# Attention in a fused fp32 block: P turned in 32x32 blocks by VectorE, multiplied with V on four row quarters, output product in two parts

## The reference, cut to what matters

```python
# 32 query heads and 4 key/value heads of width 64; windows of 128 positions, two query blocks
scores = q @ k.T                       # band: key position in (query - 128, query]
m = maximum(max(scores), sink)
p = exp(scores - m)
probs = p / (sum(p) + exp(sink - m))   # P
out = probs @ v                        # per head: [256, 64]
x = x + out.reshape(256, 2048) @ w_o
x = x + swiglu(rms_norm(x))            # gate, up: 2048 -> 5632; down: 5632 -> 2048
```

## Time and profile before

| | us |
|---|---|
| median of three runs | 1934.54 |
| the profiled execution, its own time | 1934.93 |
| its span, first to last instruction | 1933.1 |

### The profile page before, as it was taken

How to read it: one execution, slowest core, us unless ns; L and a number is a source line. 1 busy time by engine, 2 the same in 40 slices (tenths; PEclk the granted TensorE clock), 3 DMA queues, 4 the chain that set the end, 5 groups by cost and what they waited for, 6 DMA issues and landing times.

```text
span 1933.1 us, 26528 instructions
## 1 busy us (share of the span) xinstructions
PE 1918.3 (99%) x9668; PEld 1573.9 (81%) x9668; DVE 1302.0 (67%) x1852; ACT 1075.4 (56%) x1405; POOL 555.6 (29%) x616
## 2 busy tenths in 40 slices
PE   7999999999999999999999999999999999999999
PEld 6888878888888888888887778888888888888887
DVE  5799967556878888886667877555555555554443
ACT  6444466456768686875467775544444444443332
POOL 0899852306050423302400106023222222220000
PEclk9999999999999999999999999999999999999999
DMA  8666656666555555555654445666666666666665
GB/s 298 198 188 189 181 163 194 187 197 185 163 165 163 147 180 152 174 150 179 195 186 134 129 145 180 199 195 195 193 190 192 191 196 191 193 194 195 192 193 161
DMA packets 183006, 352.45 MB, mean 182 GB/s; under 512 B 11776, under 2 KB 12288, under 8 KB 182912
## 3 DMA queue, kind: packets, MB, share of 16 engines
q1 hardware_dynamic: 181488, 350.68, 60.1%
q10 hardware_dynamic: 1424, 0.53, 0.1%
HBM read 349.07 MB, written 2.10 MB: 182 GB/s over the span
## 4 chain that ended last, share of the span: by engine, by line
PE 79%; issue 6%; DVE 4%; ACT 4%; POOL 4%; DVEq 1%; POOLq 1%; ACTq 0%; DMA 0%
PE acc L508 26%; PE acc L510 25%; PE acc L509 25%; POOL kb L448 2%; POOL kf L448 1%; ACT E L959 1%; DVEq L1132 1%; DVE w_lo L1146 1%; PE T L490 1%; ACT w_hi L761 1%; PE T L709 1%; PE T L698 1%; POOLq L443 0%; DVE E L1366 0%; DVE E L1358 0%
## 5 line engine op out<-in xcount | busy, mean ns | idle before, releaser
L1146 DVE TENSOR_TENSOR w_lo<-raw,w_hi 128x1024 fp32r<-128x1024 f32 x568 | 699.1, 1234 | 538.3 <-ACT w_hi L761 530.7
L761 ACT ACTIVATE w_hi<-raw 128x1024 fp32r<-128x1024 f32 x656 | 688.4, 1057 | 601.3 <-PE acc L510 577.9
L508 PE MATMUL acc<-w_hi,h_hi 128*128 128x512 f32 x1888 | 745.2, 395 | 9.9 <-DVE w_lo L1146 9.7
L510 PE MATMUL acc<-w_hi,h_lo 128*128 128x512 f32 x1888 | 736.8, 390 | 0.0
L509 PE MATMUL acc<-w_lo,h_hi 128*128 128x512 f32 x1888 | 736.8, 390 | 0.0
L508 PEld LDWEIGHTS acc<-w_hi,h_hi 128*128 128x128 f32 x1888 | 355.3, 188 | 89.8 <-issue 14.2
L510 PEld LDWEIGHTS acc<-w_hi,h_lo 128*128 128x128 f32 x1888 | 355.2, 188 | 74.4
L509 PEld LDWEIGHTS acc<-w_lo,h_hi 128*128 128x128 f32 x1888 | 355.5, 188 | 71.2
L479 POOL COPY fT<-fq 32x256 f32<-32x256 f32 x176 | 110.8, 630 | 388.2 <-DVE fq L1599 381.3
L417 POOL TENSOR_TENSOR w_lo<-raw,w_hi 128x1024 fp32r<-128x1024 f32 x80 | 190.3, 2404 | 76.4 <-ACT w_hi L761 76.3
L1219 DVE SCALAR_TENSOR_TENSOR T<-vpad,feat,T 128x256 f32<-128x256 f32 x464 | 182.4, 478 | 0.0
(11 more groups left out here) (237 smaller groups left out, 1564.2 us busy)
## 6 DMA issues: line engine op xcount, KB each, us to landing
raw<-in_hgrn_w_in_dram SPq DMA_DIRECT2D x160, 512.0 KB, 3.7
raw<-in_conv_w_in_dram SPq DMA_DIRECT2D x96, 512.0 KB, 4.2
raw<-in_ffn_w_gate_dram SPq DMA_DIRECT2D x88, 512.0 KB, 4.4
raw<-in_ffn_w_up_dram SPq DMA_DIRECT2D x88, 512.0 KB, 4.5
raw<-in_ffn_w_down_dram SPq DMA_DIRECT2D x88, 512.0 KB, 4.8
raw<-in_attn_w_qkv_dram SPq DMA_DIRECT2D x40, 512.0 KB, 4.1
raw<-in_conv_w_out_dram SPq DMA_DIRECT2D x32, 512.0 KB, 4.6
raw<-in_hgrn_w_out_dram SPq DMA_DIRECT2D x32, 512.0 KB, 4.6
```

Of the source, the lines that this page charges most:

```text
L508: nc.tensor.matmul(o, hi[:, kt, a], w_hi[:, slot, kk, :], start=kt == 0, stop=False)
L510: last = nc.tensor.matmul(o, lo[:, kt, a], w_hi[:, slot, kk, :], start=False, stop=kt == p.chunks * CK - 1)
L761: A(w_hi[:, slot, :, :], raw[:, slot, :, :], ACT.Copy).then_inc(hi_ready, 1)
L1146: TT(w_lo[:, slot, :, :], raw[:, slot, :, :], rounded(w_hi[:, slot, :, :]), ALU.subtract).then_inc(split_ready, 1)
```

## The change

1. **P is scaled by two other engines.** `scale_p` becomes `inverse` (VectorE, reciprocal alone), `scale_first` (GpSimd, query block 0, four operations of 256 elements a group, behind its chunk e+9) and `scale_second` (ScalarE, query block 1, eight copies of 128x256 with a scale, at e+10+i).
2. **P is turned by VectorE** within 32x32 blocks (`p_turn(i)`, two transposes of 128x384 at e+11+i) straight into `PT`, which now holds all 8 heads. `turn_p` and `p_copy` go.
3. **V lies in all four row quarters.** `v_rows` on GpSimd copies V so that each quarter of the partitions holds all 8 blocks of 32 keys: 16 copies of 32x512, behind `k_turn`. `kvtok` now shares memory with PT.
4. **`mix_v(g)`** is one step for all 8 heads: 60 fp32 products (32 rows, 64 columns of the array, 128 moving columns), in turn over 4 row quarters and 2 column halves, at tick e+16 (g = 3: e+14). It waits for `masked` of group g+1, since it writes all of T.
5. **`y_out_hi(g)`** (four copies of 128x256 on ScalarE) moves to tick e+18 (g = 3: e+16), **`y_low(g)`** (four on VectorE) to e+19 (g = 3: e+17).
6. **att_out in two parts**: eight segments of 4 chunks, first the upper 1024 rows of `w_o` for the four column groups, then the lower. `first_part` (VectorE) adds the first to x. Column groups are complete after chunks 19, 23, 27 and 31 of att_out. `late` and `lead` go.

```diff
     for name, iters, per, more in (
             ("conv_ab", 4, 2, {}), ("conv_z", 1, 4, {}), ("conv_out", 1, 4, {}), ("hgrn", 4, 4, {}),
-            ("hgrn_z", 1, 4, {}), ("hgrn_out", 1, 4, {}), ("kv_q", 1, 5, {}), ("att_out", 1, 4, {"lead": 2}),
+            ("hgrn_z", 1, 4, {}), ("hgrn_out", 1, 4, {}), ("kv_q", 1, 5, {}), ("att_out", 1, 8, {"chunks": CPG // 2}),
             ("gate_up", FJ, 2, {}), ("down", 1, 4, {"chunks": FCH})):
...
-        kvtok = sb(yl2, "kvtok", [P, TB, GC])
+        PT = sb(yl2, "PT", [P, 8, 3 * P])
+        kvtok = PT[:, :, :].rearrange("p a b -> p (a b)")[:, 0:TB * GC].rearrange("p (a b) -> p a b", a=TB)
         aq = sb(yl2, "aq", [P, TB, GC])
+        vrows = apad[:, 3:5, :, :].rearrange("p a b (c d) -> p (a b c) d", d=KVH * HD)
...
-        PT = sb(yl2, "PT", [P, 4, 3 * P])
...
+            def v_rows():
+                pool.wait_ge(a_ev, 1)
+                pool.wait_ge(a_T, 1)
+                for a in range(4):
+                    for b in range(4):
+                        nc.gpsimd.tensor_copy(vrows[a * QUARTER:(a + 1) * QUARTER, b::4, :], kvtok[b * QUARTER:(b + 1) * QUARTER, :, KVH * HD:])
+                nc.gpsimd.drain().then_inc(a_rows, 1)
+
+            def scale_first(g, i):
+                pool.wait_ge(a_inv, 4 * g + i + 1)
+                nc.gpsimd.tensor_tensor(sm[:, 2 * i:2 * i + 2, P:2 * P], sm[:, 2 * i:2 * i + 2, P:2 * P],
+                                        ast[:, 6, 2 * i:2 * i + 2].unsqueeze(2).to_broadcast([P, 2, P]), ALU.mult).then_inc(a_n0, 1)
+            v_rows()
...
+                    i = n - ph["kv_q"].chunk0
+                    if i % 8 == 1:
+                        for p in range(4):
+                            scale_first(i // 8 - 3, p)
...
                 pe.wait_ge(a_cp, 2)
                 if g:
-                    pe.wait_ge(a_ptc, 8 * g)
+                    pe.wait_ge(a_sm, 8 * g)
+                if g > 1:
+                    pe.wait_ge(a_lo, 4 * (g - 1))
...
+            def mix_v(g):
+
+                pe.wait_ge(a_rows, 1)
+                pe.wait_ge(a_pt, 4 * g + 4)
+                pe.wait_ge(a_sm, 8 * (min(g + 1, 3) + 1))
+                if g:
+                    pe.wait_ge(a_lo, 4 * g)
                 for tb in range(TB):
-                    for h in (2 * i, 2 * i + 1):
-                        o = T[HD * (h % 2):HD * (h % 2) + HD, 2 + i // 2, (i % 2) * S + tb * P:(i % 2) * S + S]
-                        w = PT[:, h % 4, 2 * P:3 * P] if tb else PT[:, h % 4, 0:2 * P]
-                        last = nc.tensor.matmul(o, v(tb), w, start=tb == 0, stop=tb == 1)
+                    for step in range(5):
+                        for a in range(4):
+                            blocks = range(4 + a, 4 + a + 5) if tb else range(a + 1)
+                            if step >= len(blocks):
+                                continue
+                            b, r = blocks[step], slice(a * QUARTER, (a + 1) * QUARTER)
+                            key = b if b < 4 else b - 4
+                            for c in range(2):
+                                o = T[c * HD:(c + 1) * HD, a, :].rearrange("p (i t q) -> p i t q", t=TB, q=QUARTER)[:, 0:4, tb, :]
+                                w = PT[r, c:8:2, b * QUARTER:(b + 1) * QUARTER]
+                                last = nc.tensor.matmul(o, vrows[r, key, g * HD:(g + 1) * HD], w, start=step == 0, stop=step == len(blocks) - 1)
                 last.then_inc(a_o, 1)
...
-                for i in range(4):
-                    at.put(e + 8 + i, lambda g=g, i=i: turn_p(g, i))
-                    at.put(e + 9 + i, lambda g=g, i=i: mix_v(g, i))
+                at.put(e + 16 if g < 3 else e + 14, lambda g=g: mix_v(g))
...
+            def scale_second(g, i):
+                act.wait_ge(a_inv, 4 * g + i + 1)
                 for h in (2 * i, 2 * i + 1):
...
+                    s = probabilities(h)[1]
+                    last = A(s, s, ACT.Copy, scale=ast[:, 6, 8 + h:8 + h + 1])
+                last.then_inc(a_n1, 1)
+
+            def y_out_hi(g):
+                act.wait_ge(a_o, g + 1)
+                for i in range(4):
+                    A(by_quarters(y_hi, 4 * g + i), mixed(i).rearrange("p a (b i) -> p a b i", b=TB), ACT.Copy).then_inc(a_hi, 1)
...
-                        at.put(e + 11 + i, lambda g=g, i=i: p_copy(g, i))
-                    for b in range(2):
-                        at.put(e + 13 + 2 * b, lambda g=g, b=b: y_out_hi(g, b))
+                        at.put(e + 10 + i, lambda g=g, i=i: scale_second(g, i))
+                    at.put(e + 18 if g < 3 else e + 16, lambda g=g: y_out_hi(g))
...
+            def first_part(name, k):
+
+                dve.wait_ge(chunk_used, ph[name].done(0, k))
...
+                    if ph[name].in_parts:
+                        at.put(ph[name].last[k] + 3, lambda k=k: first_part(name, k))
...
+            def inverse(g, i):
 
                 dve.wait_ge(a_p, 4 * g + i + 1)
                 l, inv = (ast[:, r, :].rearrange("p (a b) -> p a b", a=2)[:, :, 2 * i:2 * i + 2] for r in (4, 6))
-                V.reciprocal(inv, l)
-                settle()
+                V.reciprocal(inv, l).then_inc(a_inv, 1)
+
+            def p_turn(g, i):
+
+                dve.wait_ge(a_n0, 4 * g + i + 1)
+                dve.wait_ge(a_n1, 4 * g + i + 1)
+                if g:
+                    dve.wait_ge(a_o, g)
+                else:
+                    dve.wait_ge(a_rows, 1)
                 for h in (2 * i, 2 * i + 1):
...
+                    last = V.transpose(PT[:, h, :], sm[:, h, P:4 * P])
+                last.then_inc(a_pt, 1)
+
+            def y_low(g):
+                dve.wait_ge(a_hi, 4 * g + 4)
+                for i in range(4):
+                    low(by_quarters(hy_lo, 4 * g + i), mixed(i).rearrange("p a (b i) -> p a b i", b=TB), by_quarters(y_hi, 4 * g + i), a_lo)
...
+                    at.put(e + 8, lambda g=g: masked(g, 1)).put(e + 8, lambda g=g: inverse(g, 0)).put(e + 8, lambda g=g: maxima(g, 1))
                     for i in range(1, 4):
-                        at.put(e + 9 + i, lambda g=g, i=i: scale_p(g, i))
-                    for b in range(2):
-                        at.put(e + 14 + b, lambda g=g, b=b: y_low(g, b))
+                        at.put(e + 9 + i, lambda g=g, i=i: inverse(g, i))
+                    for i in range(4):
+                        at.put(e + 11 + i, lambda g=g, i=i: p_turn(g, i))
+                    at.put(e + 19 if g < 3 else e + 17, lambda g=g: y_low(g))
```

More of the change, by code:

```diff
@@ L78, with __init__ @@
 class Phase:
-    def __init__(self, iters, per_iter, chunk0, pair0, uses0, chunks=CPG, lead=0):
+    def __init__(self, iters, per_iter, chunk0, pair0, uses0, chunks=CPG, columns=4):
         self.chunk0, self.pair0, self.uses0 = chunk0, pair0, uses0
@@ L88, in __init__, with segment, row @@
         self.uses_per = [sum(self.pair(k) == p for k in range(per_iter)) for p in range(2)]
-        head = [(k, c) for cs in (range(chunks - 4), (chunks - 4, chunks - 3), (chunks - 2,), (chunks - 1,))
-                for k in range(lead) for c in cs]
-        self.seq = head + [(k, c) for k in range(lead, per_iter) for c in range(chunks)]
+        self.seq = [(k, c) for k in range(per_iter) for c in range(chunks)]
         self.last = {k: i for i, (k, c) in enumerate(self.seq) if c == chunks - 1}
-        self.chunks = chunks
+        self.chunks, self.in_parts, self.columns = chunks, per_iter == 2 * columns, columns
         self.chunk1 = chunk0 + iters * len(self.seq)
         self.uses1 = [uses0[p] + iters * self.uses_per[p] for p in range(2)]
+    def segment(self, k):
+        return k + self.columns if self.in_parts else k
+    def row(self, k, c):
+        return self.chunks * (k // self.columns) + c if self.in_parts else c
     def pair(self, k):
@@ L106, in done, with first_reads @@
         return self.base(j) + self.last[k] + 1
+    def first_reads(self, k):
+        return k == 0 or self.in_parts and k == self.columns
     def use(self, j, k):
@@ L112, in end @@
     def end(self, k):
-        return self.last[k] + 1
+        return self.last[self.segment(k)] + 1
 def phases():
@@ L386, in _ @@
             stream("kv_q", 0, lambda k: (t["attn_w_qkv_2"][0], (k - 1) * GC if k else D))
-            stream("att_out", 0, lambda k: (t["attn_w_o_2"][0], k * GC))
+            stream("att_out", 0, lambda k: (t["attn_w_o_2"][0], k % 4 * GC))
             with sp.Fori(0, FJ) as j:
@@ L498, in stream @@
                     n, slot, _ = slots(base, i)
-                    if need is not None and k == 0:
-                        need(c)
+                    row = p.row(k, c)
+                    if need is not None and p.first_reads(k):
+                        need(row)
                     if c == 0 and not (isinstance(p.use(j, k), int) and p.use(j, k) == 0):
@@ L505, in stream @@
                     for kk, tb in ((0, 0), (1, 0), (0, 1), (1, 1)) if ends else ((0, 0), (0, 1), (1, 0), (1, 1)):
```

(6 more changed lines are left out.)

69 lines of the change are left out of this document (22 added, 47 removed).

## The result

The changed kernel takes 1962.37 us (median of four runs, 1960.96 to 1962.55); the kernel before took 1934.78 beside it. The ratio is 1.0141, 95% interval 1.0128 to 1.0153: 27.6 us slower, where 29.8 were predicted. The profiled execution's span is 1960.7 us, 27.6 more than before's.

A forecast was written before the change was run, and what follows sets the result against it. TensorE was taken as the bound, with a second chain across engines 0.8 us behind that would take over. Terms 0.7 + 14.6 + 1.2 + 4.9 + 8.4 = 29.8 us on 1934.54 gave 1964.3, range 1948 to 1983.

The forecast's parts named there:

- group 0 to 1, without clock: First period from scores to scores, with no y_out_hi in the way: 33.7 us against 33.0, +0.7.
- groups 1 to 2 and 2 to 3, without clock: Two later periods: ScalarE's wait at y_out_hi, copies and scaling lengthen each from 32.75 to 40.0 us, +7.3 twice.
- clock at three waits: TensorE's waits for rope at q_turn drop its clock: 0 to 2.8 us each, taken as 2.8 each, 8.4.
- behind scores(3): After the last scores, late w_lo of chunks 51 to 53 makes TensorE 1.2 us later at chunk 58.
- behind att_out: After the output products, TensorE waits for x_lo(2) behind GpSimd's three moves: 4.9 us, or 2.8 with moves at 10.90.
- S: Start of scores(1), 1064.11 in the earlier trace; times in the softmax chain are counted from it.
- M: Length of one mix_v on TensorE: 2.25 us if all eight tiles overlap, 6.5 if row quarters do not.
- rival one: In mix_v, row quarters do not overlap, M = 6.5: +17 us, 1981 in all; chance 0.14.
- upper bound: Top of the main case's bounds for the whole kernel: 1975 us, with M of 3 and clock lost at two more waits.
- Z: End of column group 0 in att_out; x_lo(2) was forecast at Z+49.4, wanted by TensorE at Z+44.5.
- Rival two: ScalarE's y_out_hi finds mix_v nearly done, so the chain grows by copies alone: +12 us, 1946; chance 0.09.
- the faster rival: Softmax groups: TensorE's sum decides if the second chain stays under 28.5 us: 1918 to 1923; chance 0.07.

The follow-up runs named there:

- idle-filling run: Changed kernel with 24, 32 and 20 useless 512-column matmuls on TensorE ahead of the wait in q_turn(1), (2) and (3); 1957.18 us, ratio 1.0116.
- run by quarters: Changed kernel with the same 60 products of each mix ordered one row quarter after another instead of in turn; 1971.42 us, ratio 1.0185.
- version with ScalarE's order: Changed kernel with late mix copies, GpSimd scaling P's second half, TensorE turning column group 2, V's copies split, q_out earlier, exps(3) later; 1931.06 us, ratio 0.9984.
- bursts of 240: Changed kernel with the 60 products of each mix_v made twice, the second pass writing the same result over; 1982.25 us, ratio 1.024.
- last ordered version: The version with ScalarE's order, with VectorE's third turn of P ahead of y_low and the fourth pair's reciprocal right behind the rope; 1930.63 us, ratio 0.9977.

## Why the prediction was right, point by point

| term | predicted | trace |
|---|---|---|
| ahead of scores(0) | 0 | 2.1 |
| group 0 to 1, without clock | 0.7 | 0.4 |
| groups 1 to 2 and 2 to 3, without clock | 14.6 | 13.5 |
| clock at three waits | 8.4 | 5.2 |
| behind scores(3) | 1.2 | 0.9 |
| behind att_out | 4.9 | 5.3 |
| sum | 29.8 | 27.5 |

The column on the right is stretch after less stretch before, with the clock's part from the idle-filling run's periods or, the same, q_turn to scores less 3.78 (5.71, 5.48 and 5.39 us).

**The mechanism.** Scores to scores were forecast at 33.7, 40 and 40 and are 33.4, 39.5 and 39.5 once the clock's part is taken out. The wait ahead of y_out_hi was forecast at 4.9 us, from S+8.87 to S+13.75; it is 4.96 and ends at S+13.93. VectorE goes on behind the rope at S+35.8, forecast 36.15. The experiments that moved only that step and y_low behind it moved the time both ways, so this cause is shown, not argued.

**M.** 2.25 forecast, 2.17 measured; rival one (row quarters don't overlap) is out. The run by quarters shows that it would have been right by half, had the products stood in the plain order.

**The copies.** Four copies of 128x256 from PSUM take 1.07 us to the next step, 0.27 each, not 0.36: the earlier trace rows had them with a second operand (`feat`). That is 0.4 of the 0.5 us by which each period came out shorter; the rest is the turn's start, for which the sum had 0.1 us behind VectorE's and the trace has nothing. The scaling (0.81 a pair) and p_turn(2) (0.95) came as priced.

**The clock, the term furthest off.** I carried 2.8 us over from the start of the span to each wait (by my own figures, 6.39 less 3.41, it is 3.0). The waits were 7.0, 8.9 and 4.9 us, and the loss 1.9, 1.7 and 1.6: the granted clock came back within the first chunk, while at the span's start fifteen matmuls ran low. The clock fell behind the 4.0 us for hy_lo as well (0.66 from 1131 to 1136), at no price, since q_turn(3) waited all the same. Behind the wait in gate_up I took nothing; 3.55 us of idle time brought the clock down there too, and the loss was 1.7 (PEclk 0.66 over 5 us). In all 6.9 for 8.4: two errors that offset one another by half. How near 29.8 comes to 27.6 is in part luck: 3.2 us too much here and 1.1 too much in the two long periods stand against 2.1 ahead of scores(0), for which I had nothing. The upper bound was mis-added too: 3 us for the mix and twice 2.8 for the clock make 1973, not 1975.

**v_rows.** I took 0 of the bounds 0 to 1, having read that VectorE's steps last no longer beside GpSimd's moves of 32x256. That reading was wrong: in the trace of before four w_lo in a row beside such moves start every 1.34 us and take 1.41 each, not 1.22, and a move beside a w_lo takes over three times as long:

```profile
1200.33 5.43 DVE L1146 TENSOR_TENSOR w_lo<-raw,w_hi 128x1024 fp32r<-128x1024 f32 x4
L432 POOL COPY apad<-aq x48: 387/398/1462, 1168.3 to 1204.7; 32x256 f32<-32x256 f32 x48
1169.62 1.43 POOL L432 COPY apad<-aq 32x256 f32<-32x256 f32 x1
```

(The second row has the shortest, the middle and the longest of the 48 moves in ns.) Beside copies of 32x512 three of the rope's operations took 1.09 instead of 0.68 and three of w_lo 1.35 to 1.66 instead of 1.23; v_rows costs 1.2, outside of my bounds. The other 0.8 us ahead of scores(0) stand by k_turn already, ahead of anything that the change touches; among the traces here k_turn starts anywhere from 1008.9 to 1011.0.

**The end.** 4.9 forecast, all of it wait; it is 3.6 of wait and 1.7 of clock. My terms add up to Z+49.05, not Z+49.4, so the forecast should have been 4.6. The three moves take 10.81, 11.13 and 12.05 us instead of the earlier trace rows's 10.90, 12.07 and 11.83, 0.8 less together, which is most of the rest. Their length is set by VectorE: undisturbed moves start every 0.43 us, so 16 would take 6.9 us, an estimate from these rows; four or five of each 16 take 1.3 to 1.5, each of them beside a w_lo. Rival two (ScalarE's order hurts less, 1946) and the faster rival (1918 to 1923, "a chain that is not one") didn't come; but the latter's number can't be had cheaply either: with the order mended the three groups take 32 us on the mean, not TensorE's 28.5.

## What to carry to other kernels

When an engine's program is written out in order, a step that reads another engine's result delays all that stands behind it: put it by the time at which its input is there, not by the time at which it is wanted. Before taking work from the engine that is busy for 99%, add up the next chain: here it stood 0.8 us behind, and of the some 16 us that TensorE was relieved of by its own sum (its busy time fell by 13.1 us, to 1905.2, in the version with ScalarE's order), nothing reached the time, and no more than 0.2% of it once steps on ScalarE, VectorE and GpSimd had been moved too.

## What the runs showed of the hardware

- **Tiles over row quarters and column halves work side by side.** Interleaved over four row quarters and two column halves, 120 records of 128 columns start every 18 ns on average; ordered by quarter, every 35 ns; both for fp32 products in two passes. One record takes 109 ns, so six of the eight tiles are at work on the mean, an estimate from these rows; the tiles of the longest quarter have 18 records each, 1.96 of the 2.17 us.
- **A long burst runs dry.** 231 small records passed at 17.5 ns each, then TensorE stood 2.08 us for no reason that a row shows; all four bursts of 240 did it, somewhere behind record 182 to 239, and 120 at a time don't show it. The cause is open.
- **GpSimd's copies and VectorE's operations on two tiles hold each other up.** The copy that started 0.02 us behind a w_lo, and that w_lo:

```profile
1021.97 1.23 DVE L1178 TENSOR_TENSOR w_lo<-raw,w_hi 128x1024 fp32r<-128x1024 f32 x1 [1.79 <-ACT w_hi L793]
1021.99 1.68 POOL L487 COPY apad<-PT 32x512 f32<-32x512 f32 x1
```

The w_lo took its usual 1.23 us, the copy 1.68 instead of 0.61. The rope's operations and the copies took turns: the former started every 1.02 us instead of 0.60, the latter every 1.0 to 1.1 instead of 0.65. The Trainium skill, "SBUF — State Buffer", section "Who interferes with whom", calls the ports that the two engines share an exclusive lock and has a VectorE instruction with two SBUF inputs contend with a GpSimd instruction that reads SBUF. The trace agrees, up to a part of each operation that isn't held up: one after the other would be 0.60 + 0.65 = 1.25 us, an estimate from these rows, against 1.02.
- **Idle time costs twice.** After waits of 3.6 to 8.9 us the next matmuls run at the 1.2 GHz level and lose 1.4 to 2.9 us more, and the loss doesn't follow the length of the wait: 1.4 behind 7.1 us with V's copies split, 2.9 behind 3.8 us with the copies of the mix two ticks later. Shorter waits can cost it too: 2.2 us at q_turn(1) in the last ordered version lost 1.6, 1.9 us there in the version before it lost nothing. In the last ordered version the second scores of group 2 also ran low behind a wait of 2.1 us (four of 64x256 took 0.85 us instead of 0.43). Work without use in the gap brought the clock back, 5.2 us over three gaps; and where a later wait covers it, as behind hy_lo in group 2, the fallen clock costs nothing.
